# Output projections from whole float32 operands instead of split ones, and the weight loads that follow the freed ring places

## The chip, the cores and the metric

The kernel runs on one core of one Trainium2 chip. The metric is the device time of one execution in microseconds (us), the median of three runs. A profile of one further execution shows every instruction of the five engines (TensorE or PE with its weight loads PEld, VectorE or DVE, ScalarE or ACT, GpSimd or POOL, SyncE or SP, which issues most DMAs) and the DMA traffic.

## What is computed

One inference step of a two-layer backbone over 640 tokens (512 latent, 128 context) of width 1024, all in float32. Each layer is a token mixer and a mixture of experts, each behind a norm, a modulation and a gate that come from the conditioning vectors:

```
for layer in range(DEPTH):                       # DEPTH = 2
    mp = jnp.split(cond_ctx @ mod_w[layer] + mod_b[layer], 6)   # the same for latent tokens: ms
    hp = _modulate(xp, norm1_g[layer], mp[0], mp[1])
    # layer 0: recurrent mixer;  y = (h * gelu(gate)) @ rg_w_out
    # layer 1: banded attention; y = attend(q, k, v) @ at_w_o
    xp = xp + mp[2] * yp
    xp = xp + mp[5] * _expert_choice_moe(_modulate(xp, norm2_g[layer], mp[3], mp[4]), ...)
```

The change touches the two products with `rg_w_out` and `at_w_o`, each of 640 x 1024 mixed rows with a 1024 x 1024 matrix, called output projections here.

## The kernel before

Weights flow through a ring of 12 places in SBUF (`ring`, a place is 128 x 2048 float32). SP's queue issues every load into it in an order written out by hand. A load waits on a semaphore that says that the place's last reader is done: `ring_used` counts the slices of the modulation matrices that PE has used (12 matrices `m0` to `m11`, four places each, sent in the order `MOD_ORDER`), `moe_used` the pieces of expert weights, `out_mm` the token tiles of the output projections (`NT` = 5 tiles of 128 tokens a layer). `SLOT_LOADS` lists for each third of the ring (places 0 to 3, 4 to 7, 8 to 11) what is loaded there in turn; PE waits for the matching count of `slot_ready`.

Each layer's stages, in order: modulation, turned norm, the mixer, the output projection (`mixer_out`, L749 to L768) with the residual behind it on DVE (L1478), the second norm and the router (L722 to L747), the choice of tokens on DVE (`route`, L1498), the experts (`experts`, L797). In the experts, gathers of token rows from `x_hat` on POOL's queue (L559) feed transposes on PE (`x_turn`, L832), and PE multiplies them with weight pieces of two ring places each, read in the order 8, 9, 10, 11, 0, 1, and so on.

For `mixer_out` both operands are split in two parts of fewer bits (type float32r): `mo_hi` + `mo_lo` for the mixed rows and `wo_hl` (a high and a rest part) for the weights. PE adds three products: high x high, high x rest, rest x high (L761 to L765). Who makes the parts:

- layer 0: the weights lie in ring places 8 to 11. ACT copies their high parts (`out_weights_high`, L1167) in two groups of four, the first ahead of `mod_reads([4])` on ACT's queue (L1294, L1295); POOL (L526) and DVE (L1464) subtract for the rest. ACT copies the mixed rows' high part (`mixed_high`, L1174) once `hg_ok` says that all 8 blocks of the recurrent mixer are done, DVE subtracts (`mixed_rest`, L1472).
- layer 1: POOL makes both weight parts between the units of the attention loop, a copy (L661) and a subtraction (L664) for each of 8 blocks; the mixed rows are split once the 40 units of attention are done (`o_ok`).

The split weights `wo_hl` take ring places 0 to 7, so `m5` and `m11` are loaded to places 8 to 11 as the weights there are used up, and `m6`, `m7` to places 0 to 7 when the projection is done (`out_mm`). The attention loop (L1062) keeps five units in flight: scores on PE, masked maxima on DVE (L1808) and two small DVE operations (L1812, L1814), exponentials on ACT, the scaling of the row on POOL (L652), a transpose on PE, copies on ACT and DVE, the product with the values on PE.

Between tiles 0 and 1 of a projection PE does `gate_rows` (L713): four calls that multiply a 128 x 128 and a 128 x 512 float32 operand.

Of the kernel before, what the change touches and what calls it, by code (L numbers as in the profile page):

```python
# [7 lines left out]
F32 = mybir.dt.float32  # L8
F32R = mybir.dt.float32r
# [32 lines left out]
MOD_SLOT = {0: 0, 1: 4, 2: 8, 3: 0, 4: 4, 5: 8, 6: 0, 7: 4, 9: 8, 10: 0, 8: 8, 11: 8}  # L42

SLOT_LOADS = (("m0", "w_in", "m3", "m6", "moe0", "m10", "qkv", "moe1"),
              ("m1", "w_in", "m4", "m7", "moe0", "qkv", "moe1"),
              ("m2", "w_out", "m5", "moe0", "m9", "m8", "w_o", "m11", "moe1"))
# [16 lines left out]
def build(nc, x_all, state, cache_k, cache_v, c, c_ctx, mod_w, mod_b, norm1_g, norm2_g,  # L64
# [3 lines left out]
    with ExitStack() as ctx:  # L68
# [3 lines left out]
        def sem(name):  # L72
# [28 lines left out]
        xq_hi = nc.alloc_sbuf_tensor_at("xq_hi", [P, 2, KB, P], F32R, offset=gb_at)  # L101
        wq_hi = nc.alloc_sbuf_tensor_at("wq_hi", [P, KB, D], F32R, offset=ring_at + 4 * KB * 2 * D)
# [3 lines left out]
        wo_hl = nc.alloc_sbuf_tensor_at("wo_hl", [P, KB, 2, D], F32R, offset=ring_at)  # L106
        mo_hi = nc.alloc_sbuf_tensor_at("mo_hi", [P, KB, NTOK], F32R, offset=W_at)
        mo_lo = [nc.alloc_sbuf_tensor_at("mo_lo0", [P, KB, NTOK], F32R, offset=r1_at + 4 * 5 * D),
                 nc.alloc_sbuf_tensor_at("mo_lo1", [P, KB, NTOK], F32R, offset=r1_at)]
# [132 lines left out]
        wo_hi_ok, wo_lo_ok, mo_hi_ok, mo_lo_ok = sem("wo_hi_ok"), sem("wo_lo_ok"), sem("mo_hi_ok"), sem("mo_lo_ok")  # L242
# [99 lines left out]
        def _(sp):  # L342
# [11 lines left out]
            def load_moe(layer):  # L354
# [7 lines left out]
                for n in range(8, 8 + 16, 2):  # L362
                    slot = n % SLOTS
                    if n >= 20:
                        sp.wait_ge(moe_used, LAYER_USES * layer + (n - 20) // 2 + 1)
                    elif layer == 0:

                        sp.wait_ge(ring_used, used((6, 7, 5)[slot // 4], slot + 1))
                    elif slot >= KB:
                        sp.wait_ge(ring_used, used(11, slot + 1))  # L370
                    else:

                        sp.wait_ge(out_mm, 2 * NT)
                    part(slot, int(n >= 16), 0, n % 8 // 2)
# [41 lines left out]
            load_mod(5, wo_lo_ok, lambda s: 2 * (s + 1))  # L416
            for v in (6, 7):
                load_mod(v, out_mm, lambda s: NT)
# [25 lines left out]
            load_mod(11, wo_lo_ok, lambda s: KB + 2 * (s + 1))  # L444
# [17 lines left out]
        def _(pool):  # L462
# [63 lines left out]
            for k in range(KB // 2):  # L526
                pool.wait_ge(wo_hi_ok, k + 1)
                nc.gpsimd.tensor_tensor(wo_hl[:, k, 1, :], ring[:, KB + k // 2, (k % 2) * D:(k % 2 + 1) * D],
                                        wo_hl[:, k, 0, :].bitcast(F32), ALU.subtract).then_inc(wo_lo_ok, 1)
# [117 lines left out]
            for u in range(NU):  # L647
                w = len(KEYB[units[u][0]][0]) * P

                pool.wait_ge(rs_ok, u + 1)  # L650
                pr = pms[u % 4][:, :, 0:w]
                nc.gpsimd.tensor_tensor(pr, pr, stat[:, u % 4, 6, :].unsqueeze(2).to_broadcast([P, 2, w]),  # L652
                                        ALU.mult).then_inc(pn_ok, 1)
                k, part = divmod(u - 6, 4)
                if 0 <= k < KB and part in (0, 2):

                    w = ring[:, KB + k // 2, (k % 2) * D:(k % 2 + 1) * D]
                    if part == 0:
                        pool.wait_ge(slot_ready[KB + k // 2], ready("w_o", KB + k // 2))
                        pool.wait_ge(qkv_mm, NT)  # L660
                        nc.gpsimd.tensor_copy(wo_hl[:, k, 0, :], w).then_inc(wo_hi_ok, 1)  # L661
                    else:
                        pool.wait_ge(wo_hi_ok, KB + k + 1)
                        nc.gpsimd.tensor_tensor(wo_hl[:, k, 1, :], w, wo_hl[:, k, 0, :].bitcast(F32), ALU.subtract).then_inc(wo_lo_ok, 1)  # L664
# [8 lines left out]
        def _(pe):  # L673
# [75 lines left out]
            def mixer_out(layer, after_first=None):  # L749

                for t in range(NT):
# [4 lines left out]
                    for k in range(KB):  # L757
                        if t == 0:
                            for ok in (wo_hi_ok, wo_lo_ok, mo_hi_ok, mo_lo_ok):
                                pe.wait_ge(ok, KB * layer + k + 1)  # L760
                        for x, part in ((mo_hi, 0), (mo_hi, 1), (mo_lo[layer], 0)):  # L761
                            for n in range(2):
                                mm = nc.tensor.matmul(ps[:, 2 * (t % 2) + n, :], x[:, k, toks], wo_hl[:, k, part, n * 512:(n + 1) * 512],  # L763
                                                      start=(k == 0 and x is mo_hi and part == 0),
                                                      stop=(k == KB - 1 and x is not mo_hi))  # L765
# [268 lines left out]
            for t in range(NT):  # L1034
# [6 lines left out]
                for m, k in enumerate(QKV_ORDER):  # L1041
# [5 lines left out]
                    x_hi, x_lo = xq_hi[:, t % 2, k, :], mo_lo[1][:, k, t * P:(t + 1) * P]  # L1047
# [66 lines left out]
        def _(act):  # L1114
# [52 lines left out]
            def out_weights_high(ks):  # L1167

                for k in ks:
                    act.wait_ge(slot_ready[KB + k // 2], ready("w_out", KB + k // 2))  # L1170
# [728 lines left out]
```

## Time and profile before

| What | Value |
|---|---|
| median of 3 runs | 1917.42 us (1915.45 to 1919.76) |
| the profiled execution | 1916.31 us, span 1914.5 us |
| mean granted TensorE clock in it | 0.932 of full speed |
| busy: PE, DVE, ACT, POOL | 1727.4, 603.7, 364.0, 305.0 us |
| DMA traffic | 525.09 MB, mean 274 GB/s |

Times of single instructions come from the profiled execution, counted from its span's start. A matmul's recorded duration is longer than the distance from one matmul to the next, since matmuls are pipelined; a group's length from its first start to the next group's start is what it costs. In the rows, "x48" is a count of records.

### The profile page before, as it was taken

The page shows a single profiled execution, that of the slowest core. Times are in us where ns is not written, and L with a number is a line of the kernel's source. Part 1 is how long each engine was busy: PE and PEld are TensorE (multiplying, and loading weights), DVE is VectorE, ACT ScalarE, POOL GpSimd, SP SyncE. Part 2 cuts the span into 40 slices and gives each one's busy share as a digit, 9 for nine tenths or more (in the row PEclk, how much of TensorE's full clock was granted, in tenths as well). Part 3 has the DMA queues.
Part 4 walks back from the last instruction along what each step waited for, and adds up shares of the span by engine and source line. Part 5 has one row for each costly group of instructions (what it writes and reads, how often), then busy time and mean ns, then how long its engine had stood idle before and what let it go on. Part 6 is the DMA issues. An engine that isn't in the chain of part 4 may idle for free.

```text
span 1914.5 us, 30889 instructions
## 1 busy us (share of the span) xinstructions
PE 1727.4 (90%) x13475; PEld 838.0 (44%) x13475; DVE 603.7 (32%) x1075; ACT 364.0 (19%) x723; POOL 305.0 (16%) x340
## 2 busy tenths in 40 slices
PE   5899869799999999999988788897699999999997
PEld 1788657533323323332376566576233323233322
DVE  2567663511111011011365477535201101101102
ACT  2376741100000000000231256412000000000000
POOL 1132220110110110111100167300101011101100
PEclk8899979699999999999998899895799999999999
DMA  9400542899999999999800400108599999999994
GB/s 391 130 1 1 215 191 116 356 350 393 387 407 368 394 396 381 401 408 397 347 3 1 182 23 23 45 9 364 195 402 384 406 372 392 399 375 385 409 405 165
DMA packets 57684, 525.09 MB, mean 274 GB/s; under 512 B 12352, under 2 KB 12640, under 8 KB 24783
## 3 DMA queue, kind: packets, MB, share of 16 engines
q1 hardware_dynamic: 48000, 490.63, 63.7%
q0 software_dynamic: 8176, 27.08, 5.1%
q10 hardware_dynamic: 1374, 5.37, 0.7%
q8 instruction: 112, 1.84, 0.4%
q14 instruction: 22, 0.17, 0.0%
HBM read 500.50 MB, written 22.55 MB: 273 GB/s over the span
## 4 chain that ended last, share of the span: by engine, by line
PE 80%; DVE 9%; ACT 4%; DMA 3%; issue 3%; POOL 1%; SPq 0%; DVEq 0%; ACTq 0%; POOLq 0%
PE ps L812 35%; PE ps L816 17%; PE ps L763 6%; PE ps L1050 5%; PE ps L743 2%; DMA ring<-in_rg_w_in 1%; DMA ring<-in_mod_w 1%; PE ps L952 1%; PE ps L953 1%; PE ps L954 1%; PE ps L1096 1%; PE ps L1083 1%; PE ps L1070 1%; PE ps L735 1%; PE ps L974 1%
## 5 line engine op out<-in xcount | busy, mean ns | idle before, releaser
L812 PE MATMUL ps<-ring,W 128*32 128x512 f32 x6144 | 740.2, 600 | 19.7 <-issue 18.4
L816 PE MATMUL ps<-ring,W 128*16 128x512 f32 x3072 | 403.4, 597 | 0.0
L812 PEld LDWEIGHTS ps<-ring,W 128*32 128x32 f32 x6144 | 194.6, 111 | 462.6 <-issue 460.0
L1116 ACT ACTIVATE W<-ps 128x512 f32<-128x512 f32 (+6 forms) x126 | 68.5, 561 | 920.5 <-PE ps L854 731.1
L816 PEld LDWEIGHTS ps<-ring,W 128*16 128x16 f32 x3072 | 90.9, 98 | 239.3 <-issue 239.3
L1553 DVE TENSOR_TENSOR W<-ps,amod 128x1024 f32<-128x1024 f32 (+1 forms) x32 | 28.5, 892 | 488.8 <-PE ps L839 368.8
L1562 DVE TENSOR_TENSOR W<-ps,W 128x1024 f32<-128x1024 f32 x16 | 19.6, 1225 | 278.1 <-PE ps L816 278.1
L763 PE MATMUL ps<-wo_hl,mo_hi 128*128 128x512 f32 x320 | 89.5, 403 | 12.1 <-DVE mo_lo L1475 12.1
L564 POOL DMA_INDIRECT x_mid<-W,si_l x14 | 20.2, 1445 | 377.4 <-DVE W L1573 313.0
L564 POOL DMA_INDIRECT out_y_all<-W,si_l x14 | 20.1, 1433 | 377.3 <-DVE W L1573 310.8
L1569 DVE SCALAR_TENSOR_TENSOR W<-ps,sg_l,W 128x1024 f32<-128x1024 f32 x16 | 20.5, 1284 | 182.1 <-PE ps L816 182.1
L763 PEld LDWEIGHTS ps<-wo_hl,mo_hi 128*128 128x128 f32 x320 | 62.0, 195 | 26.4 <-issue 13.5
L703 PE MATMUL ps<-ring,cond 128*2 128x512 f32 x384 | 55.0, 699 | 13.2 <-DMA ring<-in_mod_w 12.3
L1208 ACT ACTIVATE W<-ps 128x1024 f32<-128x1024 f32 x16 | 16.4, 1023 | 211.2 <-PE ps L816 211.2
L763 PE MATMUL ps<-wo_hl,mo_lo 128*128 128x512 f32 x160 | 50.6, 398 | 0.0
L1573 DVE SCALAR_TENSOR_TENSOR W<-ps,sg_c,W 16x512 f32<-16x512 f32 x64 | 47.6, 743 | 1.5
L952 PE MATMUL ps<-mx_hi,wcol_g 128*128 128x320 f32 x128 | 42.2, 329 | 6.5 <-DVE wcol_g L1669 6.5
L952 PE MATMUL ps<-mx_hi,wcol_u 128*128 128x320 f32 x128 | 40.4, 315 | 6.6 <-DVE wcol_u L1669 6.6
L1050 PE MATMUL ps<-wq,xq_hi 128*128 128x512 f32 x160 | 46.0, 412 | 0.0
L953 PE MATMUL ps<-mx_lo,wcol_g 128*128 128x320 f32 x128 | 41.6, 325 | 0.0
L954 PE MATMUL ps<-mx_hi,wcol_g 128*128 128x320 f32 x128 | 41.5, 324 | 0.0
L953 PE MATMUL ps<-mx_lo,wcol_u 128*128 128x320 f32 x128 | 40.2, 314 | 0.0
(269 smaller groups left out, 2110.9 us busy)
## 6 DMA issues: line engine op xcount, KB each, us to landing
ring<-in_moe_w_gate SPq DMA_DIRECT2D x64, 2048.0 KB, 11.1
ring<-in_moe_w_up SPq DMA_DIRECT2D x64, 2048.0 KB, 9.7
ring<-in_moe_w_down SPq DMA_DIRECT2D x64, 2048.0 KB, 12.1
ring<-in_mod_w SPq DMA_DIRECT2D x48, 1024.0 KB, 12.2
ring<-in_rg_w_in SPq DMA_DIRECT2D x8, 1024.0 KB, 27.3
ring<-in_at_w_qkv SPq DMA_DIRECT2D x8, 768.0 KB, 8.9
x_hat<-r ACTq DMA_DIRECT2D x2, 2560.0 KB, 29.0
ring<-in_rg_w_out SPq DMA_DIRECT2D x4, 1024.0 KB, 8.7
```

The costliest lines, as they stand in the source:

```text
L564: nc.gpsimd.indirect_dma_start(x_res[layer], bass.IndirectOffsetOnAxis(ap=index, axis=0), rows, None, compute_op=ALU.add).then_inc(scatter ...
L703: mm = nc.tensor.matmul(ps[g:g + 2, mod_bank(n), :], cond[:, 2 * s + k, :], ring[:, slot, k * D + h * 512:k * D + (h + 1) * 512], start=(s ...
L743: mm = nc.tensor.matmul(ps[:, 4, t * NE:(t + 1) * NE], feat(xn2)[:, k, t * P:(t + 1) * P], router[:, route, k, :], start=(k == 0 and t == ...
L763: mm = nc.tensor.matmul(ps[:, 2 * (t % 2) + n, :], x[:, k, toks], wo_hl[:, k, part, n * 512:(n + 1) * 512], start=(k == 0 and x is mo_hi a ...
L812: nc.tensor.matmul(ps[q * CG:(q + 1) * CG, bank + n, :], lat(q, k), ring[:, slots[q // 2], cols], start=(k == 0), stop=(k == KB - 1))
L816: mm = nc.tensor.matmul(ps[q * CG:q * CG + CC, bank + 2, :], ctx(a, k), ring[:, slots[a], h * D + n * 512:h * D + (n + 1) * 512], start=(k ...
L952: nc.tensor.matmul(ps[:, bank, 0:HT], w[:, 0, k, :], mx_hi[:, k, toks], start=(k == 0), stop=False)
L953: nc.tensor.matmul(ps[:, bank, 0:HT], w[:, 0, k, :], mx_lo[:, k, toks], start=False, stop=False)
L954: mm = nc.tensor.matmul(ps[:, bank, 0:HT], w[:, 1, k, :], mx_hi[:, k, toks], start=False, stop=(k == KB - 1))
L1050: mm = nc.tensor.matmul(ps[:, 3 * (t % 2) + n, :], x, w[n], start=(m == 0 and part == 0), stop=(m == KB - 1 and part == 2))
L1116: nc.scalar.activation(out, in_, ACT.Copy).then_inc(done, n)
L1573: v.scalar_tensor_tensor(out=ob_c[q // 2 * CG:q // 2 * CG + CC, q % 2 * 512:(q % 2 + 1) * 512], in0=ps[rows, bank + 2, :], scalar=sg_c[row ...
```

## The change

Both projections multiply the mixed rows and the weights as they lie, in float32: two calls for each block k of 128 rows (n = 0, 1) where there were six. All splitting of these operands goes, on ACT, DVE and POOL, with its four semaphores. PE takes the weights from ring places 8 to 11 and waits, in tile 0, for `slot_ready`, and in layer 0 for `hg_ok` block by block. Since places 0 to 7 stay free of `wo_hl`, `m5` goes to places 0 to 3, `m6` to 4 to 7, both right behind the modulations that used these places; `m7` goes to places 0 to 3 once `m5` is used, and `m11` to 0 to 3. The first expert weights of layer 0 for places 0 to 3 then wait for `m7`, and those for places 4 to 7, which wait for `m6`, stand behind them in SP's queue.

```diff
-MOD_SLOT = {0: 0, 1: 4, 2: 8, 3: 0, 4: 4, 5: 8, 6: 0, 7: 4, 9: 8, 10: 0, 8: 8, 11: 8}
-SLOT_LOADS = (("m0", "w_in", "m3", "m6", "moe0", "m10", "qkv", "moe1"),
-              ("m1", "w_in", "m4", "m7", "moe0", "qkv", "moe1"),
-              ("m2", "w_out", "m5", "moe0", "m9", "m8", "w_o", "m11", "moe1"))
+MOD_SLOT = {0: 0, 1: 4, 2: 8, 3: 0, 4: 4, 5: 0, 6: 4, 7: 0, 9: 8, 10: 0, 8: 8, 11: 0}
+
+
+SLOT_LOADS = (("m0", "w_in", "m3", "m5", "m7", "moe0", "m10", "qkv", "m11", "moe1"),
+              ("m1", "w_in", "m4", "m6", "moe0", "qkv", "moe1"),
+              ("m2", "w_out", "moe0", "m9", "m8", "w_o", "moe1"))
...
         xq_hi = nc.alloc_sbuf_tensor_at("xq_hi", [P, 2, KB, P], F32R, offset=gb_at)
+        xq_lo = nc.alloc_sbuf_tensor_at("xq_lo", [P, KB, NTOK], F32R, offset=r1_at)
-        wo_hl = nc.alloc_sbuf_tensor_at("wo_hl", [P, KB, 2, D], F32R, offset=ring_at)
-        mo_hi = nc.alloc_sbuf_tensor_at("mo_hi", [P, KB, NTOK], F32R, offset=W_at)
-        mo_lo = [nc.alloc_sbuf_tensor_at("mo_lo0", [P, KB, NTOK], F32R, offset=r1_at + 4 * 5 * D),
-                 nc.alloc_sbuf_tensor_at("mo_lo1", [P, KB, NTOK], F32R, offset=r1_at)]
...
-                for n in range(8, 8 + 16, 2):
-                    slot = n % SLOTS
+                def first(n):
+                    part(n % SLOTS, int(n >= 16), 0, n % 8 // 2)
+
+                if layer == 0:
+
+                    sp.wait_ge(out_mm, NT)
+                    first(8)
+                    first(10)
+                    load_mod(7, ring_used, lambda s: used(5, s))
+                    for n in range(12, 20, 2):
+                        sp.wait_ge(ring_used, used((7, 6)[n // 16], n % SLOTS + 1))
+                        first(n)
+                else:
+
+                    sp.wait_ge(out_mm, 2 * NT)
+                    first(8)
+                    first(10)
+                    for n in (12, 14):
+                        sp.wait_ge(ring_used, used(11, n % SLOTS + 1))
+                        first(n)
+                for n in (20, 22) if layer == 0 else ():
+                    sp.wait_ge(moe_used, (n - 20) // 2 + 1)
+                    first(n)
+                for n in (16, 18, 20, 22) if layer == 1 else ():
                     if n >= 20:
-                        sp.wait_ge(moe_used, LAYER_USES * layer + (n - 20) // 2 + 1)
-                    elif layer == 0:
-
-                        sp.wait_ge(ring_used, used((6, 7, 5)[slot // 4], slot + 1))
-                    elif slot >= KB:
-                        sp.wait_ge(ring_used, used(11, slot + 1))
-                    else:
-
-                        sp.wait_ge(out_mm, 2 * NT)
-                    part(slot, int(n >= 16), 0, n % 8 // 2)
+                        sp.wait_ge(moe_used, LAYER_USES + (n - 20) // 2 + 1)
+                    first(n)
...
             sp.wait_ge(mod_tr, 5)
             sp.dma_start(tok(r1)[:, 3:NT, :], x_tiles[:, 3:NT, :]).then_inc(x_in, 16)
-            load_mod(5, wo_lo_ok, lambda s: 2 * (s + 1))
-            for v in (6, 7):
-                load_mod(v, out_mm, lambda s: NT)
+            for v in (5, 6):
+                load_mod(v, ring_used, lambda s: used(v - 2, s))
             store_x(0, r1)
             load_moe(0)
...
-            load_mod(11, wo_lo_ok, lambda s: KB + 2 * (s + 1))
+            load_mod(11, qkv_mm, lambda s: NT)
             store_x(1, r2)
             load_moe(1)
...
-            for k in range(KB // 2):
-                pool.wait_ge(wo_hi_ok, k + 1)
-                nc.gpsimd.tensor_tensor(wo_hl[:, k, 1, :], ring[:, KB + k // 2, (k % 2) * D:(k % 2 + 1) * D],
-                                        wo_hl[:, k, 0, :].bitcast(F32), ALU.subtract).then_inc(wo_lo_ok, 1)
...
                 pr = pms[u % 4][:, :, 0:w]
                 nc.gpsimd.tensor_tensor(pr, pr, stat[:, u % 4, 6, :].unsqueeze(2).to_broadcast([P, 2, w]),
                                         ALU.mult).then_inc(pn_ok, 1)
-                k, part = divmod(u - 6, 4)
-                if 0 <= k < KB and part in (0, 2):
-
-                    w = ring[:, KB + k // 2, (k % 2) * D:(k % 2 + 1) * D]
-                    if part == 0:
-                        pool.wait_ge(slot_ready[KB + k // 2], ready("w_o", KB + k // 2))
-                        pool.wait_ge(qkv_mm, NT)
-                        nc.gpsimd.tensor_copy(wo_hl[:, k, 0, :], w).then_inc(wo_hi_ok, 1)
-                    else:
-                        pool.wait_ge(wo_hi_ok, KB + k + 1)
-                        nc.gpsimd.tensor_tensor(wo_hl[:, k, 1, :], w, wo_hl[:, k, 0, :].bitcast(F32), ALU.subtract).then_inc(wo_lo_ok, 1)
...
                         pe.wait_ge(out_mul, 2 * (NT * layer + t - 1))
                     toks = slice(t * P, (t + 1) * P)
                     for k in range(KB):
+                        slot = KB + k // 2
                         if t == 0:
-                            for ok in (wo_hi_ok, wo_lo_ok, mo_hi_ok, mo_lo_ok):
-                                pe.wait_ge(ok, KB * layer + k + 1)
-                        for x, part in ((mo_hi, 0), (mo_hi, 1), (mo_lo[layer], 0)):
-                            for n in range(2):
-                                mm = nc.tensor.matmul(ps[:, 2 * (t % 2) + n, :], x[:, k, toks], wo_hl[:, k, part, n * 512:(n + 1) * 512],
-                                                      start=(k == 0 and x is mo_hi and part == 0),
-                                                      stop=(k == KB - 1 and x is not mo_hi))
+                            if layer == 0:
+                                pe.wait_ge(hg_ok, k + 1)
+                            pe.wait_ge(slot_ready[slot], ready(("w_out", "w_o")[layer], slot))
+                        for n in range(2):
+                            mm = nc.tensor.matmul(ps[:, 2 * (t % 2) + n, :], feat((r2, r1)[layer])[:, k, toks],
+                                                  ring[:, slot, k % 2 * D + n * 512:k % 2 * D + (n + 1) * 512],
+                                                  start=(k == 0), stop=(k == KB - 1))
                     mm.then_inc(out_mm, 1)
                     if t == 0 and after_first is not None:
                         after_first()
...
-                    x_hi, x_lo = xq_hi[:, t % 2, k, :], mo_lo[1][:, k, t * P:(t + 1) * P]
+                    x_hi, x_lo = xq_hi[:, t % 2, k, :], xq_lo[:, k, t * P:(t + 1) * P]
...
-            def out_weights_high(ks):
-
-                for k in ks:
-                    act.wait_ge(slot_ready[KB + k // 2], ready("w_out", KB + k // 2))
-                    act.wait_ge(ring_used, used(3 + k // 4, k))
-                    copy(wo_hl[:, k, 0, :], ring[:, KB + k // 2, (k % 2) * D:(k % 2 + 1) * D], wo_hi_ok)
-
-            def mixed_high(layer):
-
-                if layer == 0:
-                    act.wait_ge(hg_ok, KB)
-                else:
-                    act.wait_ge(o_ok, NU)
-                for k in range(KB):
-                    copy(mo_hi[:, k, :], feat((r2, r1)[layer])[:, k, :], mo_hi_ok)
...
                     nc.scalar.activation(gel[:, HT:], ps[:, 3, 0:HT], ACT.Gelu_apprx_tanh).then_inc(gel_ok, 1)
-            out_weights_high(range(KB // 2))
             mod_reads([4])
-            mixed_high(0)
-            out_weights_high(range(KB // 2, KB))
             gate_copy(0, gb)
             squares(1, 0)
             mod_reads([5], turn_last=False)
...
-            mixed_high(1)
...
-            def out_weights_rest():
-
-                eng.wait_ge(wo_lo_ok, KB // 2)
-                for k in range(KB // 2, KB):
-                    eng.wait_ge(wo_hi_ok, k + 1)
-                    v.tensor_tensor(wo_hl[:, k, 1, :], ring[:, KB + k // 2, (k % 2) * D:(k % 2 + 1) * D],
-                                    wo_hl[:, k, 0, :].bitcast(F32), ALU.subtract).then_inc(wo_lo_ok, 1)
-
-            def mixed_rest(layer):
-                for k in range(KB):
-                    eng.wait_ge(mo_hi_ok, KB * layer + k + 1)
-                    v.tensor_tensor(mo_lo[layer][:, k, :], feat((r2, r1)[layer])[:, k, :], mo_hi[:, k, :].bitcast(F32),
-                                    ALU.subtract).then_inc(mo_lo_ok, 1)
...
-            mixed_rest(0)
-            out_weights_rest()
             diagonals(0, diag)
             eng.wait_ge(x_in, 48)
...
-                v.tensor_tensor(mo_lo[1][:, :, cols], feat(r1)[:, :, cols], xq_hi[:, t % 2].bitcast(F32), ALU.subtract).then_inc(xq_lo_ok, 1)
+                v.tensor_tensor(xq_lo[:, :, cols], feat(r1)[:, :, cols], xq_hi[:, t % 2].bitcast(F32), ALU.subtract).then_inc(xq_lo_ok, 1)
...
-            mixed_rest(1)
             diagonals(1, diag1)
             residual(1, r2, gb1)
```

## Rows read from the trace of the kernel before

**Rows 1.** The page's shares of the chain that ended last.
```profile
PE 80%; DVE 9%; ACT 4%; DMA 3%; issue 3%; POOL 1%; SPq 0%; DVEq 0%; ACTq 0%; POOLq 0%
```

**Rows 2.** Windows: length, busy us of PE, PEld, DVE, ACT, POOL; clock; DMA share, GB/s.
```profile
600.00:700.00 100.00, 100.00 (x928) 31.15 (x924) 17.30 (x20) 3.13 (x4) 11.08 (x14) 1.00 1.00 391
1113.80:1220.60 106.80, 85.67 (x846) 63.48 (x842) 76.48 (x291) 64.51 (x231) 75.71 (x50) 0.96 0.11 38
260.00:262.00 2.00, 1.79 (x4) 1.50 (x5) 2.00 (x4) 2.00 (x4) 0.00 (x0) 0.50 0.00 0
262.00:264.00 2.00, 2.00 (x8) 1.58 (x7) 2.00 (x4) 2.00 (x4) 0.00 (x0) 0.74 0.00 0
1230.00:1232.00 2.00, 2.00 (x7) 1.52 (x6) 2.00 (x4) 0.05 (x1) 0.00 (x0) 0.50 0.00 0
1232.00:1235.00 3.00, 3.00 (x14) 2.46 (x13) 2.01 (x2) 0.00 (x0) 0.00 (x0) 0.93 0.00 0
```

**Rows 3.** Chain in order of time, layer 0's projection: start us, us, what.
```profile
260.21 12.50 PE ps L763 x48
272.71 3.44 PE ps L718 x8
276.14 43.54 PE ps L763 x192
```

**Rows 4.** Timeline ahead of it: start us, us, engine, line, operation, out<-in.
```profile
242.10 3.88 ACT L1116 ACTIVATE wo_hl<-ring 128x1024 fp32r<-128x1024 f32 x4
243.22 11.98 POOL L528 TENSOR_TENSOR wo_hl<-ring,wo_hl 128x1024 fp32r<-128x1024 f32 x4 [5.14 <-ACT wo_hl L1116]
245.88 0.57 ACT L1116 ACTIVATE r<-ps 128x512 f32<-128x512 f32 x1
...
250.25 0.18 ACT L1116 ACTIVATE modraw<-ps 128x16 f32<-128x16 f32 x1 [3.72 <-PE ps L688]
...
257.61 0.82 DVE L1720 TENSOR_TENSOR r<-W 128x640 f32<-128x640 f32 x1
```

**Rows 5.** Chain in order of time, layer 1's projection.
```profile
1224.92 0.74 ACT mo_hi L1116
...
1226.73 13.82 PE ps L763 x48
...
1243.98 43.54 PE ps L763 x192
```

**Rows 6.** Chain, attention loop: first and last of eight long L1812 pieces.
```profile
1122.69 1.71 DVE stat L1812
...
1215.70 1.52 DVE stat L1812
```

**Rows 7.** The tile wo_hl: durations in ns, minimum, median, maximum.
```profile
L664 POOL TENSOR_TENSOR wo_hl<-ring,wo_hl x8: 2349/2364/2368, 1122.0 to 1214.8; 128x1024 fp32r<-128x1024 f32 x8
```

**Rows 8.** POOL's timeline in the attention loop (units 3, 5, 24 and 28).
```profile
1104.39 1.47 POOL L652 TENSOR_TENSOR gb<-gb,stat 128x768 f32<-128x768 f32 x1 [0.97 <-DVE stat L1821]
...
1110.34 1.47 POOL L652 TENSOR_TENSOR W<-W,stat 128x768 f32<-128x768 f32 x1 [1.00 <-DVE stat L1821]
...
1180.90 1.47 POOL L652 TENSOR_TENSOR W<-W,stat 128x768 f32<-128x768 f32 x1 [1.01 <-DVE stat L1821]
...
1193.96 1.47 POOL L652 TENSOR_TENSOR W<-W,stat 128x768 f32<-128x768 f32 x1 [1.01 <-DVE stat L1821]
```

**Rows 9.** Timeline at the start of layer 0's experts.
```profile
382.27 23.87 SPq L358 DMA_DIRECT2D ring<-in_moe_w_up  x4
...
393.38 0.87 POOL L560 DMA_INDIRECT W<-x_hat,gi_c  x1 [0.30 <-issue]
...
398.40 1.04 PE L816 MATMUL ps<-ring,W 128*16 128x512 f32 x8
...
399.38 1.09 PE L839 MATMUL ps<-ident,W 128*128 128x128 f32 x8
```

**Rows 10.** Line L560, gathers issued from 391 to 395 us.
```profile
DMA to landing us min/median/max: 5.4/5.5/5.6
```

**Rows 11.** Line L560, gathers issued from 411 to 416 us.
```profile
DMA to landing us min/median/max: 7.6/8.4/9.2
```

## What the change should do to the time

> **What bounds the kernel now.** I read the page first, for the shares of the chain that ended last, then the windows by stage, then the chain in order of time around each projection. The chain is PE for 80% of its length [rows 1]. In the experts PE has no idle time while the weights arrive at 391 GB/s [rows 2], so both PE's work and the lead of the loads matter there. Around the projections the chain runs through nothing but PE: tile 0, the gate rows, four more tiles [rows 3, 5]. The attention loop is different: PE is busy 85.67 of 106.8 us there, and DVE, ACT and POOL lie between 64 and 77 us [rows 2]; it is a loop of short waits between four engines, where a delay on any of them can reach the end. So three things decide: what a tile costs PE, when tile 0 can start, and what the work that leaves POOL was holding up.
>
> **What a tile costs.** Four tiles take 43.54 us in each layer [rows 3, 5], so 10.89 us a tile. That is 48 calls, 192 records for four tiles, so one record a call and 0.227 us for each. The new form has 16 calls a tile. Their price is in the gate rows: four calls of the same shape with whole float32 operands leave 8 records and take 3.44 us [rows 3]. So a float32 call is two records of 0.43 us, 0.86 us, against 0.68 us for the three split calls that it replaces. A tile becomes 16 x 0.86 = 13.76 us, 2.87 us more. A third of the calls is no saving. Tiles 1 to 4 of both layers: 8 x 2.87 = **+23.0 us**. Weight loads of 128 columns are in the price already, since the gate rows have the same operand shape. The residual on DVE behind the tiles has more time than before and stays hidden.
>
> The Trainium skill (FP8 and Floating Point Precision, TensorE Precision Notes) says that true FP32 takes four passes through the array. The trace agrees in kind: 0.86 us is 3.8 times 0.227 us. If each pass cost as much as a split call here, a tile would be 14.5 us and the whole sum 7.6 us higher than by the row.
>
> **Tile 0 in layer 0.** Now it ends at 272.71 us [rows 3]; it starts at 260.21 us because the mixed rows are split only when the last block is done at 258.43 us [rows 4]. After the change it waits only for PE's predecessor, the modulation row that ACT has copied out at 250.43 us. ACT makes that copy behind four copies of the output weights, 242.10 to 245.88 us [rows 4]; without them all of it comes 3.78 us earlier, so PE is free at 246.65 us. Blocks 0 to 6 are ready by then (the load of these weights itself waited for block 6 with `hg_ok`, at L407). Block 7 is asked for after 14 calls, 12.0 us or more later, at 258.7 us at the earliest, when the last block is just done even at today's time. And POOL's four subtractions, which ran beside that block's work on DVE from 243.22 to 255.2 us, go. The clock is the open point: the stretch is entered after idling, at half clock (the lower level, 1.2 GHz, granted 0.50). In layer 0 the half clock lasted from 260.2 to about 263 us, in layer 1 from 1226.7 to about 1232.3 us [rows 2], 2.8 and 5.5 us; half of such a stretch is lost, 1.4 to 2.8 us. I take 2.0. Tile 0 ends at 246.65 + 13.76 + 2.0 = 262.4 us: **-10.3 us** (-10.9 to -9.5). That cover matters: were PE held to 258.43 us, the term would be +1.5 us.
>
> **Tile 0 in layer 1.** The split mixed rows cost 1224.92 to 1226.73 us [rows 5]; that wait goes, 1.8 us. The tile took 13.82 us, 2.9 of them lost to the low clock. The new one: 13.76 plus 2.5 us. 1224.92 + 16.26 = 1241.2 against 1240.55 us: **+0.6 us** (-0.5 to +1.0).
>
> **The attention loop.** POOL's eight copies and eight subtractions go. A subtraction holds POOL 2.36 us [rows 7]. On the chain, L1812, an operation on 128 x 2 numbers that takes 0.17 us otherwise, takes 0.93 to 1.71 us in eight places [rows 6], once beside each subtraction; in order they are 1.71, 0.93, 0.93, 0.93, 0.98, 1.08, 1.20 and 1.52, 9.28 us in all. Without the subtractions that is 9.28 - 8 x 0.17 = 7.9 us less on the chain. The pace says the same by another way: two units without copies and subtractions took 5.95 us, 2.98 each; four like them with one of each 13.06 us, 3.27 each [rows 8], 1.2 us for a group whose long L1812 was 0.8 us too long. Between 7.9 and 1.4 times that I take **-9 us**. Bounds: nothing, if another wait of the loop takes the place; and the full length of the subtractions, 8 x 2.36 = 18.9 us.
>
> The Trainium skill (SBUF — State Buffer, Who interferes with whom) has DVE and GpSimd share a port pair that is locked for a whole instruction, when DVE reads two operands in SBUF and GpSimd reads SBUF. L1812 does that. The trace shows waits below that length, 1.5 us at most beside 2.36, since L1812 comes when part of the subtraction is over. By the full length of the lock the sum would be 9.9 us lower.
>
> **The loads.** `m5`, `m6` and `m11` come earlier and `m7` goes behind the first four places of expert weights; none is late, as `m7` has from the residual's end to 380 us. What is late is next in SP's queue. Now two expert parts (places 4 to 7) are issued from 382.27 us on, when `m7` is being used; after the change four (places 0 to 3, and 4 to 7 behind them), each of two places, 2.1 MB, or 5.4 us at 391 GB/s [rows 2]. They end near 404 us instead of 393. PE reads places 8 to 11 first, 10 us of work, so places 0 to 3 are there 10 us ahead of use. But the second gather, issued until 394.25 us [rows 9], travels beside them. Now it lands 5.5 us after issue [rows 10], and PE's transposes for it start at 399.38 us, without a gap behind the group that ended at 399.44 [rows 9]: no slack at all. Under full load gathers took 7.6 to 9.2 us [rows 11], 2.1 to 3.7 us more. I take **+2.5 us** (0 to +5). `m11` and the first parts in layer 1 have no such neighbour: nothing.
>
> Taken away at no price: ACT's and DVE's splitting behind `hg_ok` and `o_ok`, four semaphores, PE's waits on them. They lie ahead of tile 0 and are in its two terms.
>
> **The sum.** 23.0 - 10.3 + 0.6 - 9 + 2.5 = **+6.8 us**. The profiled execution would go from 1916.31 to 1923.1 us; it lies 1.1 us below the median, so the median goes from 1917.42 to **1924.2 us**. A measurement of this kernel can tell about 0.2%, 3.8 us, from no change: 1913.6 to 1921.3 is the same.
>
> **Rivals.**
> - *A float32 call is one record's work* (the gate rows' 8 records would be something else). Then a tile is 6.9 us, 6.9 us less on each of ten tiles: 1924.2 - 69 = 1855 us, faster. It decides if calls, not records, cost 0.43 us. Against it: 3.44 us for four calls [rows 3]. Chance 0.02.
> - *The attention loop gives back more.* The lock hides other delays too, and the loop draws near PE's own work: up to 21 us lie between PE's busy time and the stretch [rows 2]. With 12 to 18.9 us back instead of 9, the time is 1914 to 1921 us; with over 19.6 us it is faster. For it: the pace falls by more than the long pieces. Against: the stretches without extra POOL work are not at PE's pace either, 2.98 us a unit [rows 8]. Chance 0.25, a fifth of it faster.
> - *The attention loop gives back nothing*, because the next waits on ACT take over: 1924.2 + 9 = 1933 us. Against it: the faster pace of the undisturbed units [rows 8]. Chance 0.11.
> - *The four parts come too late*, places 4 to 7 stall PE for one part, 5.4 us, or the clock falls in it: 1930 to 1935 us. Against it: 10 us of lead. Chance 0.06.
> - *The gains ahead of the tiles cancel the price* in full, without anything above: low clocks at their short ends, no gather wait, all small terms on the good side: 1919 to 1921 us. Chance 0.08, counted as the same.
>
> **How the numbers follow.** The forecast, 1921 to 1929 us, holds 0.48. With the rivals: faster 0.02 + 0.05 = 0.07; the same 0.20 + 0.08 = 0.28, and 0.02 of the forecast's low edge, 0.30; slower 0.46 + 0.11 + 0.06 = 0.63. Extremes of all terms together would be -8 and +19 us; for 8 in 10 I cut at 1916, inside the second rival, and at 1932, short of the third.
>
> **What would show it.** L763's successor with 32 records a tile, 13.7 us from tile to tile in both layers. In layer 0 its first record near 247 us, tile 0 done near 262, the last tile near 321 us (now 319.7). In the attention loop no L1812 above 0.6 us, and the loop some 9 us shorter. PE waiting 2 to 3 us for the second gather. The prediction is wrong if a tile takes under 11 or over 15 us, if tile 0 of layer 0 waits for its last block or its weights, or if the attention loop keeps its length.

## The result, and the profile after

The changed kernel takes 1938.78 us (median of four executions, 1934.17 to 1942.32) against 1917.82 us for the kernel before in the same comparison: a ratio of 1.0107, with a 95% interval of 1.0084 to 1.0130. It is some 21 us slower, where 6.8 were forecast and 1932 us was the upper end of the range. The profiled execution is the shortest of the four, 1934.17 us with a span of 1932.3, against 1914.5 before: 17.8 us to account for.

The projections first. The chain in order of time in layer 0, then in layer 1 (start us, us, what), answers to [rows 3, 5]:

```profile
247.18 15.43 PE ps L758 x32
262.61 3.43 PE ps L712 x8
266.04 54.95 PE ps L758 x128
...
1228.29 16.39 PE ps L758 x32
1244.68 3.43 PE ps L712 x8
1248.11 54.95 PE ps L758 x128
```

L758 is the call that was L763. Four tiles are 128 records and 54.95 us, 13.74 us a tile (forecast 13.76). Tile 0 of layer 0 starts 13 us earlier and is done at 262.61 (forecast 262.4). The windows of that stretch (columns as in [rows 2]) show the half clock that was allowed for:

```profile
247.00:249.00 2.00, 1.82 (x2) 0.84 (x3) 1.97 (x5) 0.13 (x1) 0.24 (x1) 0.50 1.04 418
249.00:251.00 2.00, 2.00 (x5) 0.95 (x4) 1.97 (x5) 0.00 (x0) 0.00 (x0) 0.73 1.02 406
251.00:253.00 2.00, 2.00 (x6) 0.81 (x5) 2.00 (x2) 0.00 (x0) 0.00 (x0) 1.00 1.07 438
```

The attention loop: the small DVE step of [rows 6], now L1771, in ns (minimum, median, maximum). No long piece is left.

```profile
L1771 DVE SCALAR_TENSOR_TENSOR stat<-stat,sinks x40: 160/161/586, 1107.5 to 1222.0; 128x2 f32<-128x2 f32 x40
```

The loop's length is taken from POOL's first to its last scaling of a row, before (1097.90 to 1220.52 us) and after (1109.72 to 1223.86 us):

```profile
1097.90 1.47 POOL L652 TENSOR_TENSOR W<-W,stat 128x768 f32<-128x768 f32 x1 [4.22 <-DVE stat L1821]
...
1220.52 0.61 POOL L652 TENSOR_TENSOR gb<-gb,stat 128x256 f32<-128x256 f32 x1 [0.52 <-DVE stat L1821]
```
```profile
1109.72 1.47 POOL L657 TENSOR_TENSOR W<-W,stat 128x768 f32<-128x768 f32 x1 [4.94 <-DVE stat L1780]
...
1223.86 0.61 POOL L657 TENSOR_TENSOR gb<-gb,stat 128x256 f32<-128x256 f32 x1 [0.52 <-DVE stat L1780]
```

The start of layer 0's experts, against [rows 9, 10]: the timeline, and where the second pair of gathers (L565, issued from 394.30 us) landed.

```profile
384.93 2.04 SPq L354 DMA_DIRECT2D ring<-in_moe_w_gate  x2
387.02 15.99 SPq L354 DMA_DIRECT2D ring<-in_moe_w_up  x3
...
389.11 1.09 PE L834 MATMUL ps<-ident,W 128*128 128x128 f32 x8
...
395.63 0.87 POOL L565 DMA_INDIRECT W<-x_hat,gi_c  x1 [0.30 <-issue]
...
409.54 1.97 PE L834 MATMUL ps<-ident,W 128*128 128x128 f32 x8 [6.91 <-DMA W<-x_hat,gi_c]
```
```profile
DMA to landing us min/median/max: 11.4/12.6/13.9
```

Here the forecast breaks. Four parts are issued together at 385 us, the second gather behind them lands after 11.4 to 13.9 us instead of 5.5, and PE stands 6.91 us for it. It starts again at half clock (granted 0.50 from 409.5 to 411.5 us): the transposes (L834) take 1.97 us instead of 1.09.

Stage by stage, from the two profiles (lengths in us):

| stage | before | after | difference | forecast |
|---|---|---|---|---|
| start to the end of layer 0's projection | 319.7 | 321.0 | +1.3 | +1.2 |
| to the transposes for the first gather | 67.6 | 68.1 | +0.6 | 0 |
| to the transposes for the second gather | 12.1 | 20.4 | +8.3 | +2.5 |
| rest of layer 0's experts, to `m8` | 534.0 | 534.2 | +0.2 | 0 |
| to POOL's first operation of the attention loop | 164.6 | 166.0 | +1.4 | 0 |
| to its last one | 122.6 | 114.1 | -8.5 | -9 |
| to the end of layer 1's projection | 67.0 | 79.2 | +12.2 | +12.1 |
| to the end | 627.0 | 629.3 | +2.3 | 0 |

Between these two profiles three stages are as forecast; the second gather is 5.8 us worse, and 4.5 us appear in stages that no term covers.

### The profile page after: what moved, and what is told of

Its sections match the earlier page's. It is cut to its first block, busy times and chain, and to the rows that moved or that the text cites. A ratio compares the mean times of both kernels' runs of the same rounds, so it can differ in the third digit from the quotient of the medians.

```text
span 1932.3 us, 30471 instructions
## 1 busy us (share of the span) xinstructions
PE 1760.4 (91%) x13315; PEld 810.6 (42%) x13315; DVE 570.9 (30%) x1055; ACT 345.9 (18%) x699; POOL 266.4 (14%) x320
## 4 chain that ended last, share of the span: by engine, by line
PE 79%; DVE 7%; DMA 6%; ACT 3%; issue 3%; POOL 1%; SPq 0%; DVEq 0%; POOLq 0%; ACTq 0%
PE ps L807 33%; PE ps L811 16%; PE ps L758 7%; PE ps L1045 5%; DMA W<-x_hat,gi_c 2%; PE ps L737 2%; DMA ring<-in_rg_w_in 1%; PE ps L1078 1%; PE ps L1091 1%; DMA ring<-in_mod_w 1%; PE ps L1065 1%; PE ps L947 1%; PE ps L949 1%; PE ps L948 1%; DMA out_y_all<-W,si_c 1%
## 5 line engine op out<-in xcount | busy, mean ns | idle before, releaser
L807 PE MATMUL ps<-ring,W 128*32 128x512 f32 x6144 | 742.8, 601 | 19.8 <-issue 18.5
L758 PE MATMUL ps<-ring,r 128*128 128x512 f32 x320 | 142.0, 606 | 0.6 <-ACT r L1111 0.4
L758 PEld LDWEIGHTS ps<-ring,r 128*128 128x128 f32 x320 | 62.3, 196 | 78.8 <-issue 77.7
L697 PE MATMUL ps<-ring,cond 128*2 128x512 f32 x384 | 57.7, 734 | 11.7 <-DMA ring<-in_mod_w 10.3
L947 PE MATMUL ps<-mx_hi,wcol_u 128*128 128x320 f32 x128 | 40.5, 317 | 7.0 <-DVE wcol_u L1630 7.0
L949 PE MATMUL ps<-mx_hi,wcol_u 128*128 128x320 f32 x128 | 40.2, 314 | 0.0
## 6 DMA issues: line engine op xcount, KB each, us to landing
ring<-in_moe_w_up SPq DMA_DIRECT2D x64, 2048.0 KB, 10.3
ring<-in_moe_w_down SPq DMA_DIRECT2D x64, 2048.0 KB, 12.2
ring<-in_mod_w SPq DMA_DIRECT2D x48, 1024.0 KB, 14.2
```

Of the source, the lines that this page charges most:

```text
L697: mm = nc.tensor.matmul(ps[g:g + 2, mod_bank(n), :], cond[:, 2 * s + k, :], ring[:, slot, k * D + h * 512:k * D + (h + 1) * 512], start=(s ...
L758: mm = nc.tensor.matmul(ps[:, 2 * (t % 2) + n, :], feat((r2, r1)[layer])[:, k, toks], ring[:, slot, k % 2 * D + n * 512:k % 2 * D + (n + 1 ...
L807: nc.tensor.matmul(ps[q * CG:(q + 1) * CG, bank + n, :], lat(q, k), ring[:, slots[q // 2], cols], start=(k == 0), stop=(k == KB - 1))
L947: nc.tensor.matmul(ps[:, bank, 0:HT], w[:, 0, k, :], mx_hi[:, k, toks], start=(k == 0), stop=False)
L949: mm = nc.tensor.matmul(ps[:, bank, 0:HT], w[:, 1, k, :], mx_hi[:, k, toks], start=False, stop=(k == KB - 1))
```

## The experiments

**The changed kernel again** (`e0`), to tell its steady part from chance.

> The changed kernel once more, to tell its steady part from chance. Theory A (the second gather of layer 0's experts is late because four parts of expert weights are issued together just ahead of it): the profile has PE waiting 6 to 8 us for that gather again, and the median is 19 to 22 us over the kernel before. Rival B (that wait was chance in one execution): the wait is under 2 us in this profile, and the median lies elsewhere.

Measured: 1936.16 us against 1916.49 for the kernel before, ratio 1.0111 (1.0089 to 1.0132). PE waited 7.5 us for the same gather. Theory A stands: it was no chance of one execution. The profiled one was at the short end again (1933.48), so the typical loss is about 20 us, not 17.8.

**The order of two loads** (`e1`):

```diff
-                    for n in range(12, 20, 2):
+                    for n in (16, 18, 12, 14):
                         sp.wait_ge(ring_used, used((7, 6)[n // 16], n % SLOTS + 1))
                         first(n)
```

> The changed kernel with one order turned round: the two parts for places 4 to 7, which wait for m6 alone, are issued ahead of the two for places 0 to 3, which wait for m7. Theory A (late gather under four parts): PE's wait of 6.9 us for the second gather falls under 1 us, the clock stays up, and the time is 8 to 9 us below the changed kernel, some 1929 to 1931 us. Rival B (the time was lost to the calls' price or to weights that come late): no change within 2 us. Rival C (the other two parts alone are enough to delay the gather): half of the gain, 3 to 5 us.

Measured: 1927.01 us, 9.2 us below `e0`, which was measured beside it. In its timeline two parts go at 364.38 us and only two are left beside the gather; PE does not wait:

```profile
364.38 3.28 SPq L354 DMA_DIRECT2D ring<-in_moe_w_up  x2
385.41 2.04 SPq L354 DMA_DIRECT2D ring<-in_moe_w_gate  x2
...
403.06 1.09 PE L834 MATMUL ps<-ident,W 128*128 128x128 f32 x8
```
```profile
DMA to landing us min/median/max: 5.5/5.7/5.9
```

Theory A holds in full; rivals B and C fall. In all eight profiles in which two parts travel beside the second gather it landed after 4.5 to 6.2 us, in all six with four parts after 11.0 to 14.2 us.

**The same delay without any of the change** (`e4`): the kernel before, with one wait changed.

```diff
-                        sp.wait_ge(ring_used, used((6, 7, 5)[slot // 4], slot + 1))
+                        sp.wait_ge(ring_used, used((7, 7, 5)[slot // 4], slot + 1))
```

> The kernel before, with its split operands, and one wait changed: the two parts for places 0 to 3 wait for m7 as the two for places 4 to 7 do, so that all four are issued at 382 us, as in the changed kernel. Theory A (the four parts delay the second gather, whatever the projection does): PE waits 6 to 8 us for the gather, the time is 8 to 10 us over the kernel before, some 1925 to 1926 us. Rival B (the delay needs something else of the change): no change within 2 us. Prediction's own size: 2.5 us.

Measured: 1927.22 us against 1918.21: +9.0 us, with the projections as they were. Its second gather, then PE:

```profile
DMA to landing us min/median/max: 11.0/12.3/13.6
```
```profile
406.11 1.97 PE L839 MATMUL ps<-ident,W 128*128 128x128 f32 x8 [7.11 <-DMA W<-x_hat,gi_c]
```

From the first transposes (385.68 us) to these it is 20.43 us, as in the changed kernel (20.0 to 21.3 us in the six profiles with four parts, 12.1 to 13.5 us in the eight with two). So this loss belongs to the loads alone.

**One layer at a time** (`e2`: layer 0 as changed, layer 1 as before; `e3` the reverse). In outline, for `e2`:

```diff
                     for k in range(KB):
                         slot = KB + k // 2
+                        if layer == 1:
...
+                            for x, part in ((mo_hi, 0), (mo_hi, 1), (mo_lo1, 0)):
...
+                            continue
```

> Full precision in layer 0 alone; layer 1 splits its operands as before. Theory A: the projection of layer 0 costs 1.3 us, the late gather 8 to 9, the attention loop gives nothing: 10 to 11 us over the kernel before, 1928 us. Rival B (the calls' price is larger than the tile shows, or something else in layer 0 is lost): over 13 us. If the two layers are independent, this and the run with layer 1 alone add up to the change, 19 to 22 us.

> Full precision in layer 1 alone; layer 0 splits its operands and loads as before. Theory A: four tiles cost 11.5 us more, tile 0 0.6 to 1, the attention loop gives 8.5 back: 3 to 5 us over the kernel before. Rival D (layer 1's experts lose as well, as the last 2.8 us of the profile hint): 6 to 9 us over it, with PE waiting for gathers in layer 1's experts.

Measured, both against 1916.49: layer 0 alone 1930.08, +13.6 us; layer 1 alone 1921.19, +4.7. Together +18.3, against 19.7 for the change: within the intervals of these runs the layers add up, though 19 to 22 was expected. Layer 1 is as theory A has it. Layer 0 is 3 us above its 10 to 11 and just past rival B's bound, with an interval of 9 to 17; its profile has the gather's wait (8.0 us), the projection's end 2.5 us later than before, and 3.2 us more from the end of layer 1's projection to the end of the kernel, although layer 1 is computed as before.

**POOL's work put back** (`e5`), and the same with a second copy for each subtraction (`e7`). The results are not used.

```diff
+                k, part = divmod(u - 6, 4)
+                if 0 <= k < KB and part in (0, 2):
+                    w = ring[:, KB + k // 2, (k % 2) * D:(k % 2 + 1) * D]
...
+                        nc.gpsimd.tensor_copy(spare[:, k, :], w).then_inc(wo_hi_ok, 1)
...
+                        nc.gpsimd.tensor_tensor(spare[:, k, :], w, spare[:, k, :].bitcast(F32), ALU.subtract).then_inc(wo_lo_ok, 1)
```

> The changed kernel, with POOL's eight copies and eight subtractions of the attention loop put back; their results go to free places and are not used. If they alone held up the loop, it goes from 114.1 back to some 122.6 us and the time is 8 to 9 us over the changed kernel, some 1945 us. Rival (the loop became shorter by m11's earlier load or the places): within 2 us of the changed kernel.

> As the run with POOL's work put back, but each subtraction, which reads two operands, is a second copy, which reads one; the results are not used. If it is the two-operand subtraction that holds up DVE's small steps, the loop keeps its 114 us or gains 2 at most, and no small step of DVE passes 0.7 us. If it is POOL's lost time, the loop grows by 4 us or more, as a copy's 1.04 us is to the subtraction's 2.36 us.

Measured against 1918.21: 1945.83 with the subtractions, 1940.43 with copies. The loop takes 120.7 and 115.3 us, against 114.1. The small DVE step, here L1785, is at most 1.71 us long with subtractions and 0.59 with copies. One meeting of each, from the timelines, first beside a subtraction, then beside a copy:

```profile
1134.54 2.35 POOL L672 TENSOR_TENSOR spare<-ring,spare 128x1024 fp32r<-128x1024 f32 x1
...
1135.20 1.71 DVE L1785 SCALAR_TENSOR_TENSOR stat<-stat,sinks 128x2 f32<-128x2 f32 x1
```
```profile
1136.95 1.04 POOL L672 CAST spare<-ring 128x1024 fp32r<-128x1024 f32 x1
...
1137.64 0.38 DVE L1785 SCALAR_TENSOR_TENSOR stat<-stat,sinks 128x2 f32<-128x2 f32 x1
```

In both the step ends with POOL's operation: 1136.91 against 1136.89, 1138.02 against 1137.99. So the step is held until POOL is through, by a copy too; the two operands that the expectation made the cause are not. Its numbers came true, its reason did not. A copy is shorter and met late, so the price of all of them is 1.2 us. The rule that the prediction took from the Trainium skill (SBUF — State Buffer, Who interferes with whom) fits both. What is put back is 6.6 us, less than the 8.5 gained: the loop of 122.6 us in the profile before is long for its code, which took 121.1 us in the profiles of `e4` and `e9` and 120.7 us in that of `e2`.

**Full precision where it pays** (`e6`): tile 0 alone, in both layers, with the loads of the kernel before.

```diff
                         if t == 0:
-                            for ok in (wo_hi_ok, wo_lo_ok, mo_hi_ok, mo_lo_ok):
-                                pe.wait_ge(ok, KB * layer + k + 1)
+                            if layer == 0:
+                                pe.wait_ge(hg_ok, k + 1)
+                            pe.wait_ge(slot_ready[slot], ready(("w_out", "w_o")[layer], slot))
+                            for n in range(2):
+                                mm = nc.tensor.matmul(ps[:, n, :], feat((r2, r1)[layer])[:, k, toks],
...
+                            continue
+                        if t == 1:
+                            for ok in (wo_hi_ok, wo_lo_ok, mo_hi_ok, mo_lo_ok):
+                                pe.wait_ge(ok, KB * layer + k + 1)
```

ACT's copies for the split come behind `mod_reads([4])` in layer 0 and behind the attention loop in layer 1; DVE subtracts there, after `diagonals`. The loads of `m5` and `m11`, whose places tile 0 now reads, wait for tile 0 as well.

> The kernel before, with its loads, and full precision in tile 0 of each projection alone. Tiles 1 to 4 stay split; the splitting is done beside tile 0, by ACT and DVE in layer 1, with nothing left of it on POOL in the attention loop. By the changed kernel's profile: tile 0 of layer 0 gives 10 us, the attention loop 8.5, tile 0 of layer 1 costs 0.6: 18 us under the kernel before, some 1899 us. Rival (the splits are not done when tile 1 wants them, or the gather becomes late): PE waits behind the gate rows, and the gain is under 12 us.

Measured: 1913.38 us against 1918.21, only 4.8 us gained, and not by the rival's way. At the end of layer 1's projection (1269.3 us, before 1287.5) it is 18.2 us ahead. From there to the end it loses 11 us, 9.5 of them at two places in layer 1's experts. These are a loop of three passes over two pairs each, and two pairs behind it. From one pair to the next it is 65.6 us within a pass; where the loop jumps back (a turn, in the expectations below) it is 71.6 and 71.6 us in the kernel before, and 77.1 and 75.7 here. The timelines of the first jump, before and here (PE's lines, with the wait ahead in brackets):

```profile
1538.92 3.00 PE L812 MATMUL ps<-ring,W 128*32 128x512 f32 x16 [4.13 <-issue]
```
```profile
1520.37 2.65 PE L813 MATMUL ps<-ring,W 128*32 128x512 f32 x10 [3.61 <-issue]
1526.11 1.07 PE L813 MATMUL ps<-ring,W 128*32 128x512 f32 x3 [3.09 <-issue]
```

Every jump back costs some 4 us in which PE waits for nothing that the profile shows. Here PE stops a second time, after 10 records (5 calls) of a group of 16, for 3.09 us, and stays at half clock (granted 0.50 from 1522 to 1530 us). The Trainium skill (Runtime: NRT & Kernel Launch, Instruction fetch mechanics) says that an engine's code comes by DMA in blocks of 256 instructions, and that a taken branch to a target outside the blocks at hand waits for its block. If the loop's head lies near the end of a block, two blocks may have to be waited for. That is theory E.

```diff
+            for _ in range(80):
+                pe.wait_ge(consts, 1)
             pe.wait_ge(o_ok, NU)
             mixer_out(1, lambda: gate_rows(1, diag1))
```

> As the run with full precision in the first tiles alone, but PE's program is 40 instructions longer ahead of the loop over layer 1's experts (80 waits on a semaphore that has long been reached, two to an instruction, at the end of the attention loop, where PE waits anyway). Theory E (in that run two turns of this loop took 77.1 and 75.7 us instead of some 71.6 because PE, 3.6 us after the turn, stood a second time for 3.1 us in the middle of a group, for code, and at half clock; where the loop's head lies in the program decides it): both turns take 71 to 72.5 us, and the time is 9 to 10 us lower, some 1904 us. Rival (the second stand is for weights, or comes from the earlier start): no change.

> The kernel before, with nothing but 201 instructions of PE more (satisfied waits, while PE waits for the routing of layer 1), which puts the head of the loop over layer 1's experts where it lay, by count modulo 256, in the run with full precision in the first tiles. Theory E: its two turns take 75 to 77 us instead of 71.6, and the time is 8 to 11 us over the kernel before, some 1927 us. Rival: turns as before, at most 2 us for the instructions themselves.

> The changed kernel with the two parts for places 4 to 7 issued early, and in addition PE's program 64 instructions longer ahead of the loop over layer 1's experts. Theory E: its turns, 73.1 and 72.5 us without this, take 71 to 72 us, and the time is 1 to 3 us lower, some 1925 us, which leaves 5 to 8 us over the kernel before: the price of the tiles less what tile 0 and the attention loop give. Rival: no change.

Measured against 1916.96: `e8` 1902.97, 14.0 us below, where `e6` was 4.8 below; turns 71.2 and 71.8 us. `e9` 1928.96, +12.0 us, turns 76.7 and 75.9, so 9.4 us of it lie in the turns; the stretch ahead of the experts, where the waits stand, is 2.7 us longer, more than the 2 us allowed for them. The second stop has come in `e9` after the same ten records, and is gone in `e8`. First `e9`, then `e8`:

```profile
1540.46 2.80 PE L812 MATMUL ps<-ring,W 128*32 128x512 f32 x10 [3.63 <-issue]
1545.64 1.07 PE L812 MATMUL ps<-ring,W 128*32 128x512 f32 x3 [2.39 <-issue]
```
```profile
1526.68 2.55 PE L813 MATMUL ps<-ring,W 128*32 128x512 f32 x16 [3.67 <-issue]
```

The queue that carries code (DMA view, 14 us around that turn: packets, MB, share) shows three packets in `e9`, two in `e8`. Over 30 us around the turn both have four, so this tells when code came, not that there was more of it.

```profile
q8 instruction: 3, 0.05, 1.3%
```
```profile
q8 instruction: 2, 0.03, 0.8%
```

For these two it is shown that the place of the code decides: counted in the traces, PE has 17782 instructions ahead of layer 1's experts in `e9` and 17526 in `e6`, 256 apart. That code comes in blocks of 256, no run here shows by itself. `e10` missed: 1927.87, no gain on `e1` (1927.01). Its turns did become shorter, 72.4 and 71.6 us for 73.1 (0.5 of it a wait for a gather) and 72.5, 1.7 us in all; but its 128 waits took 5.9 us where they stand (from POOL's last operation to the projection 10.3 us, 4.4 without them). In `e8` the 80 took 3.6.

**The waits where PE waits anyway** (`e11`): `e8` with the 80 waits ahead of `chosen(1)`.

```diff
+            for _ in range(80):
+                pe.wait_ge(consts, 1)
             chosen(1)
             experts(1)
```

> As the run with full precision in the first tiles and PE's program moved by 40 instructions, but the 80 waits stand where PE waits some 7 us for the routing of layer 1's experts, not at the end of the attention loop, where they took 3.6 us (from the last POOL operation to the projection 8.0 us, against 4.4). If the price was theirs, that stretch is 4.4 us again and the time is 3 to 4 us lower, some 1899 us; if not, no change. The loop's turns stay at 71 to 72 us.

Measured: 1898.61 us against 1918.39, ratio 0.9898 (0.9882 to 0.9915), 5.8 us better against its kernel before than `e8` was. That stretch is 4.4 us, 3.6 less; the turns are 71.3 and 71.7. Its chain in the two projections shows tile 0 at the new price and four tiles at the old:

```profile
247.31 15.47 PE ps L755 x32
262.77 3.43 PE ps L709 x8
266.21 43.56 PE ps L764 x192
```
```profile
1208.02 16.38 PE ps L755 x32
1224.40 3.43 PE ps L709 x8
1227.84 43.55 PE ps L764 x192
```

It beats both kernels: 19.8 us below the one before, where the changed kernel was 19.7 above it (`e0`).

## Why the prediction was wrong

The direction was right, the size was not: +6.8 us forecast, about 20 measured.

- *What a tile costs*: right, 13.74 us for 13.76. A float32 call is two records.
- *Tile 0 in layer 0*: right, done at 262.61 for 262.4. It started 0.5 us later than forecast and lost 1.7 us to the half clock where 2.0 were allowed.
- *Tile 0 in layer 1*: right against the profile before, too good against others. From POOL's last operation to its end it is 20.8 us, before 20.0: +0.8 for +0.6. But the old tile took 13.82 us only in that profile; in `e2`, `e4` and `e9`, whose layer 1 is split as before, it took 12.5 to 12.7, with the half clock over after about 3 us in `e4` and `e9` instead of 5.5. Against them the term is +1.9 to +2.1, outside its bound of +1.0. The chain of `e4`:

```profile
1232.98 12.52 PE ps L763 x48
```
- *The attention loop*: right in place and mechanism, -8.5 for -9. By the other profiles of the old code (120.7 to 121.1 us) the lasting gain is nearer 7, under the 7.9 of the long pieces alone. `e7` adds that the length of POOL's operation sets the price, not its two operands.
- *The loads*: **the step that failed**, "I take +2.5 us (0 to +5)". The place and the mechanism were right, that the second gather travels beside four parts and has no slack. The term was mis-sized: 8.3 us in the profile, 9.2 by taking it away (`e1`), 9.0 by putting it into the old kernel (`e4`), outside both ends. Two things made it small. The price under load was read from one pair of gathers (8.4 us, [rows 11]), when the profile before held a better one. Its gathers issued between 420 and 940 us, and those between 1390 and 1900 us, ten each:

```profile
DMA to landing us min/median/max: 4.3/11.3/13.8
```
```profile
DMA to landing us min/median/max: 9.3/11.5/14.5
```

  And the step added the difference in landing alone; PE, once it has stood for 7 us, starts at half clock, 0.9 us more in the transposes alone. An estimate from the four parts comes nearer: 8.4 MB from 385 us on, at the 400 GB/s of this stretch, are done at 406, and the two gathers issued among them landed at 405.7 and 409.5.
- *Parts that come too late* (chance 0.06, 1930 to 1935 us) came nearest in time, but by another way: no weights were late.
- *What no term held.* With the load term at 8.3 the sum is 23.0 - 10.3 + 0.8 - 8.5 + 8.3 = +13.3 of the profile's 17.8. The other 4.5 us are 0.6, 0.2, 1.4 and 2.3 us in stages that the change does not compute differently. With the other profiles' values for tile 0 of layer 1 and the loop, +2.0 and -6.8, the sum is +16.2 of the 19.7 that the medians show: these two, read from one profile, hide 2.9 us. A part of what is left is the loop's turn in layer 1: in the five profiles with the changed kernel's program for PE (the first, `e0`, `e1`, `e5`, `e7`) it is 72.8 us in the mean, against 71.8 in the two with the program of before (the first and `e4`), 2 us for two turns. In all five PE stands a second time behind the first jump, 0.50 to 1.04 us, at the same place, 25 records after it started again; in neither of the two, nor in `e10`, does it (in `e5` also behind the second jump, 2.49 us). The changed kernel's:

```profile
1559.56 1.49 PE L807 MATMUL ps<-ring,W 128*32 128x512 f32 x12 [0.62 <-issue]
```

  By the same count, modulo 256, these five have the loop's head 26 instructions earlier than `e6` and `e9`, and their second stop comes after 25 records instead of 10, a record being a weight load and a matmul, so 30 instructions later in the loop, which is about the same place in the program; every other program has the head 38 to 149 later, and no second stop. So 0.5 to 1.0 us (3.5 in `e5`) is the code's place. That the rest of the 2 us is too is argued, since turns differ by as much between profiles of one program. The other 2.5 to 3 us stay open.

## What to carry to other kernels

Price a transfer on a loaded queue by the work queued ahead of it and by the slowest like it in the profile; if it has no slack, move the load, since an order of two lines was worth 9 us. A dearer instruction that needs no preparation pays where it replaces waiting, in the first tile, and not in the tiles behind it. After any edit look at what the turns of later loops cost before judging the edit: the same change was worth 5 or 20 us, some 10 us of that by where a loop's code lay. And read a term from more than one profile: two that came from a single one hid 2.9 us here.

## What the hardware showed unexpectedly

- Where PE's loop jumps back, a pair took 71.6 us instead of 65.6, 6 us more, in the good case and 10 to 11.5 us more in the bad one, by where the loop's head lies in PE's program. 201 more instructions ahead of it, all satisfied waits, made the kernel before 12 us slower, 9.4 of it in two turns.
- A satisfied wait on PE is not free: 80 took 3.6 us, 128 took 5.9, 45 ns each. Where PE stood for the routing anyway, 80 of them cost nothing that shows (`e11`).
- A gather on POOL's queue landed after 4.5 to 6.2 us beside two parts of 2.1 MB (eight profiles) and after 11.0 to 14.2 us beside four (six).
